# Recurrence of a hybrid decoder layer: chunks of 64 tokens per head in place of chunks of 32 per pair of heads

## What is computed

```python
def step(state, inp):
    r_t, w_t, k_t, v_t, a_t, b_t = inp
    sa = jnp.einsum('bhvk,bhk->bhv', state, a_t)
    state = (state * w_t[:, :, None, :] + sa[..., None] * b_t[:, :, None, :]
             + v_t[..., None] * k_t[:, :, None, :])
    y_t = jnp.einsum('bhvk,bhk->bhv', state, r_t)
    return state, y_t
...
y = rwkv7_recurrence(r_h, hs(decay), k_mod, v_h, -kk, kk * alpha_h)
mean = jnp.mean(y, axis=-1, keepdims=True)
var = jnp.mean(jnp.square(y - mean), axis=-1, keepdims=True)
y = ((y - mean) * lax.rsqrt(var + GN_EPS) * f(ln_x_w).reshape(RWKV_HEADS, HEAD_DIM)
     + f(ln_x_b).reshape(RWKV_HEADS, HEAD_DIM))
bonus = jnp.sum(r_h * k_mod * f(r_k), axis=-1, keepdims=True) * v_h
return (y + bonus).reshape(bsz, t_len, RWKV_WIDTH) * g
```

## Time and profile before

| | us |
|---|---|
| three executions | 2338.67, 2337.99, 2333.99 |
| their median | 2337.99 |
| span of the profiled execution | 2329.1 |
| the median less that span | 8.9 |
| busy in the span: TensorE | 2231.0 (96%) |
| VectorE | 1756.5 (75%) |
| ACT | 1141.8 (49%) |
| GpSimd | 1025.4 (44%) |

### The profile page before, as it was taken

One profiled execution on the slowest core, in us unless ns is written; L12 is line 12 of the kernel. 1 busy time (PEld: TensorE's weight loads), 2 busy tenths in 40 slices (PEclk: granted clock), 3 DMA queues, 4 the chain that ended last, 5 costly groups with the idle time before them and its releaser, 6 DMA issues.

```text
span 2329.1 us, 43634 instructions
## 1 busy us (share of the span) xinstructions
PE 2231.0 (96%) x16652; PEld 1816.6 (78%) x16652; DVE 1756.5 (75%) x1910; ACT 1141.8 (49%) x1795; POOL 1025.4 (44%) x726
## 2 busy tenths in 40 slices
PE   7999999996999979998999999999999999999998
PEld 6777777775878768887888888788788888887886
DVE  3756798994884466769989999666799898976565
ACT  5646556452445554444444444454554444444543
POOL 4636466571234335535776766100146555541000
PEclk9999999998999989999999999999999999999999
DMA  7364556347567547895434343677733332326774
GB/s 203 93 227 134 178 160 209 106 140 216 154 166 194 144 144 234 268 279 166 153 119 147 121 146 128 217 252 255 237 119 115 104 111 93 113 95 202 247 260 145
DMA packets 435819, 395.61 MB, mean 170 GB/s; under 512 B 59548, under 2 KB 352076, under 8 KB 432332
## 3 DMA queue, kind: packets, MB, share of 16 engines
q1 hardware_dynamic: 407804, 343.06, 47.8%
q10 hardware_dynamic: 27856, 50.34, 6.0%
HBM read 266.97 MB, written 126.35 MB: 169 GB/s over the span
## 4 chain that ended last, share of the span: by engine, by line
PE 55%; DVE 3%; DMA 2%; ACT 1%; issue 1%; SPq 0%; ACTq 0%; POOLq 0%; POOL 0%; DVEq 0%
PE late_bank L133 18%; PE late_bank L134 18%; PE late_bank L135 18%; DVE wt_lo L2906 1%; DMA scratch_a<-p_keep 1%; ACT wt_hi L2727 1%; PE late_bank L2199 1%; DMA o_lo<-scratch_q 0%; DVE wt_lo L2860 0%; DMA p_keep<-in_w_down 0%; DMA raw<-in_w_down 0%; DMA scratch_x<-x_tile 0%; DMA p_keep<-scratch_td 0%; DVE p_ub L2869 0%; DVE x_tile L2168 0%
## 5 line engine op out<-in xcount | busy, mean ns | idle before, releaser
L133 PE MATMUL late_bank<-o_hi,wt_hi 128*128 128x512 f32 x1232 | 481.3, 391 | 8.0 <-DVE o_lo L2962 3.3
L134 PE MATMUL late_bank<-o_lo,wt_hi 128*128 128x512 f32 x1232 | 480.7, 390 | 0.0
L135 PE MATMUL late_bank<-o_hi,wt_lo 128*128 128x512 f32 x1232 | 480.6, 390 | 0.0
L431 POOL TENSOR_TENSOR p_w_lo<-p_w_raw,p_w_hi 128x1024 fp32r<-128x1024 f32 x72 | 190.4, 2645 | 221.2 <-ACT p_w_hi L502 221.2
L133 PEld LDWEIGHTS late_bank<-o_hi,wt_hi 128*128 128x128 f32 x1232 | 232.0, 188 | 58.7 <-issue 7.2
L135 PEld LDWEIGHTS late_bank<-o_hi,wt_lo 128*128 128x128 f32 x1232 | 232.1, 188 | 48.8
L134 PEld LDWEIGHTS late_bank<-o_lo,wt_hi 128*128 128x128 f32 x1232 | 232.0, 188 | 47.8
L2597 POOL TENSOR_TENSOR tsum<-raw 128x512 f32<-128x512 f32 x43 | 106.2, 2469 | 358.5 <-DVE p_ub L2947 179.4
L133 PE MATMUL p_ppr<-p_hT_hi,p_w_hi 128*128 128x512 f32 x576 | 233.4, 405 | 0.2 <-ACT p_ring L513 0.2
L133 PE MATMUL late_bank<-wt_hi 128*128 128x512 f32 x572 | 223.2, 390 | 7.2 <-DVE wt_lo L2906 6.6
L135 PE MATMUL p_ppr<-p_hT_hi,p_w_lo 128*128 128x512 f32 x576 | 226.6, 393 | 0.0
(11 more groups left out here) (328 smaller groups left out, 4679.3 us busy)
## 6 DMA issues: line engine op xcount, KB each, us to landing
raw<-in_w_up SPq DMA_DIRECT2D x88, 512.0 KB, 5.1
p_w_raw<-in_w_in SPq DMA_DIRECT2D x72, 512.0 KB, 3.9
scratch_a<-p_keep SPq DMA_DIRECT2D x22, 1280.0 KB, 4.5
raw<-scratch_a SPq DMA_DIRECT2D x96, 256.0 KB, 3.0
raw<-scratch_td SPq DMA_DIRECT2D x52, 256.0 KB, 3.7
p_keep<-scratch_a SPq DMA_DIRECT2D x47, 256.0 KB, 2.9
scratch_a<-p_keep SPq DMA_DIRECT2D x44, 256.0 KB, 2.0
raw<-in_w_down SPq DMA_DIRECT2D x44, 256.0 KB, 4.1
```

The source lines that it names most:

```text
L133: nc.tensor.matmul(out, lhs_hi, rhs_hi, start=start, stop=False, skip_group_check=again)
L134: nc.tensor.matmul(out, lhs_hi, rhs_lo, start=False, stop=False, skip_group_check=again)
L135: return nc.tensor.matmul(out, lhs_lo, rhs_hi, start=False, stop=stop, skip_group_check=again)
L431: nc.gpsimd.tensor_tensor(w_lo[i][:, :, :], w_raw[i][:, :, :], w_hi[i][:, :, :].bitcast(F32), ALU.subtract).then_inc(s_wl, 1)
```

## The change

Chunks are 64 tokens long (`L = 2 * C`) and every product is of one head. The array is used as four tiles of 64x64: half h of the partitions into half h of a bank is an "own" tile, the other two go crosswise. The chain's step has one more link, since `w` is gone: `from_state` gives a S + A' v, ACT takes it as `pz`, the inverse is applied, ACT takes u, `to_state`. There are two such steps in an iteration for four. In each of them the chain's eight products (own tiles) come first and eight others (the cross tiles) right behind: k v into the state's bank, A'' v into y, the gram of r and k. VectorE's `advance` is an add and a multiplication by the decay in both steps. The inverse of 64 is put together from two of 32: X21 = X2 L21 X1, in `corner`, `corner_right` and `corner_left`, with ACT taking `l21`, `m1` and `x21`, and VectorE making a 32x32 `transpose` x1u.

Order of one iteration on TensorE:

```diff
                     if b:
-                        wait_read(pe, i - 1, "w1")
                         from_state(0)
+                    if o or a2:
+                        from_r_and_gram_of_a()
+                    if b or o:
+                        inverse_first()
                     if a2:
-                        bk_transposes(0)
...
+                        corner()
+                    if d:
+                        turn_y()
+                    if b or o:
+                        to_state_first()
                     if o:
-                        from_r(0)
...
+                        from_u()
                     if b:
                         from_state(1)
                     if a2:
-                        bk_transposes(1)
...
+                        corner_right()
+                    if b or a2:
+                        inverse_second()
                     if a2:
-                        bk_transposes(2)
...
+                        gram_of_b_and_turn_k()
+                    if b or a2:
+                        to_state_second()
                     if a2:
...
+                        turn_b_and_z()
+                        corner_left(0)
+                        corner_left(1)
```

The new products, 8 of each in a chain step and 16 of each in the interleaved groups:

```diff
+                    def from_state(c2):
...
+                        for j in range(PAIRS):
+                            for h in range(2):
+                                own = nc.tensor.matmul(pbank[half(h), c2 * PAIRS + j, :], ar[now][half(h), j, 0, tokens(c2)],
+                                                       st[p][c2][half(h), j, :], start=False, stop=True, skip_group_check=True)
+                        own.then_inc(s_as, 1)
+                        for j in range(PAIRS):
+                            for h in range(2):
+                                kv = nc.tensor.matmul(sbank[half(h), j, :], bkt[p][other(h), 1, (c2 * PAIRS + j) * H:(c2 * PAIRS + j + 1) * H],
+                                                      uv[now][other(h), 1, c2 * PAIRS + j, :], start=j == 0, stop=False, skip_group_check=True)
...
+                    def from_r_and_gram_of_a():
...
+                                for h in range(2):
+                                    if o:
+                                        own = nc.tensor.matmul(ybank[half(h), c2 * PAIRS + j, :], ar[old][half(h), j, 1, tokens(c2)],
+                                                               st[q][c2][half(h), j, :], start=c2 + j == 0, stop=False, skip_group_check=True)
+                                    if a2:
+                                        ak = nc.tensor.matmul(units(AB)[other(h), c2 * PAIRS + j, :], kinds[half(h), j, 1, tokens(c2)],
+                                                              ar[nxt][half(h), j, 0, tokens(c2)], start=True, stop=True)
```

GpSimd's body (the eight copies with padding are gone):

```diff
+                    if c:
+                        n = i - 2
+                        gp.wait_ge(s_mean, ONE + n + 1)
+                        nc.gpsimd.tensor_tensor(y[n % 3][:, :, :], y[n % 3][:, :, :], stat[p][:, 0, :].unsqueeze(2).to_broadcast([P, HEADS, H]),
+                                                ALU.add).then_inc(s_yc, 1)
...
+                        gp.wait_ge(s_yc, ONE + n + 1)
+                        nc.gpsimd.tensor_tensor(y2[:, :, :], y[n % 3][:, :, :], y[n % 3][:, :, :], ALU.mult).then_inc(s_sq, 1)
...
+                        nc.gpsimd.tensor_tensor(m[:, :, :], m[:, :, :], bg[n % 2][:, :, 0, :], ALU.add).then_inc(s_add, 1)
...
+                        nc.gpsimd.tensor_tensor(m[:, :, :], m[:, :, :], bg[n % 2][:, :, 1, :], ALU.mult).then_inc(s_mo, 1)
+                    if c:
+                        n = i - 2
+                        gp.wait_ge(s_rec, ONE + n + 1)
+                        nc.gpsimd.tensor_tensor(y[n % 3][:, :, :], y[n % 3][:, :, :], stat[p][:, 3, :].unsqueeze(2).to_broadcast([P, HEADS, H]),
+                                                ALU.mult).then_inc(s_yc2, 1)
```

ACT's square (L1459) is gone. VectorE's masks are three of 128x512, its solver has `GAPS = 6` and `TURNS = 5`, so 27 parts of a block lie in five iterations (i = 0 to 4 and 5 to 9). Loads, in `phase_recur`:

```diff
+                    for h in range(2):
+                        for e in range(2):
+                            sp.dma_start(xt[g][quad(h, e), :, C * e:C * e + C], whole[k, g, h, e]).then_inc(s_xl[n % 2], 16)
+                            for c in range(2):
+                                sp.dma_start(xd[n % 2][quad(h, c), e, :, :], parts[k, g, h, c, e]).then_inc(s_xl[n % 2], 16)
...
+                            sp.dma_start(rows(bk[n % 2]), group("bk", n)).then_inc(s_in[n % 2], 16)
+                            if n >= BATCH:
+                                sp.wait_ge(s_yd, ONE + 3 * (n - BATCH + 1))
+                            sp.dma_start(rows(ar[n % BATCH]), group("ar", n)).then_inc(s_in[n % 2], 16)
+                            spread(n)
```

b with k, a with r, and bonus with gate are now one load each, from scratch laid out by group; v has two loads an iteration, the turned a none. y has three buffers for two, the mix, bonus with gate, and the norm's statistics two for one. In `phase_project` the turned rows of a are not made:

```diff
-                        if f == 1 and b > 0:
-                            a_rows(b - 1, [pm[:, g, :] for g in range(TT)])
...
-                    if pair == 0 and b > 0:
-                        pe.wait_ge(s_abr, ONE + b)
-                        rows(dec, [pm[:, g, :] for g in range(TT)], s_atn)
...
-                rows(dec, LAST, s_atn)
```

More of the change, by code:

```diff
@@ L1273, in body @@
[L1273 to L1283 removed]
+                            sp.wait_ge(s_xz, ONE + BATCH + 1)
@@ new lines, in from_r_and_gram_of_a, with from_u @@
+                        if o:
+                            own.then_inc(s_yd, 1)
+                        if a2:
+                            ak.then_inc(s_gd, 1)
+                    def from_u():
+                        pe.wait_ge(s_yd, ONE + 3 * (i - 1) + 2)
+                        for c2 in range(2):
+                            for j in range(PAIRS):
+                                for h in range(2):
+                                    u = c2 * PAIRS + j
+                                    last = nc.tensor.matmul(ybank[half(h), u, :], ark[(i - 1) % 3][half(h), 0, c2, j, :], uv[old][half(h), 0, u, :],
+                                                            start=False, stop=True, skip_group_check=True)
+                        last.then_inc(s_yd, 1)
@@ new lines, in place_of, with corner @@
+                    def place_of(name):
+                        t, k = job(i, name)
+                        pe.wait_ge(s_read[t], ONE + k)
+                        return bank[:, ROT[t], :], s_full[t]
+                    def corner():
+                        at, full = place_of("l21")
+                        for j in range(PAIRS):
+                            for c2 in range(2):
+                                for h in range(2):
+                                    last = nc.tensor.matmul(at[quad(h, c2), j * C:(j + 1) * C], ar[nxt][half(h), j, 0, c2 * L + C:c2 * L + L],
+                                                            kinds[half(h), j, 0, c2 * L:c2 * L + C], start=True, stop=True)
+                        last.then_inc(full, 1)
@@ new lines, in corner_right @@
+                    def corner_right():
+                        wait_read(pe, i, "l21")
+                        at, full = place_of("m1")
+                        pe.wait_ge(s_xu, ONE + i + 2)
+                        for j in range(PAIRS):
+                            for c2 in range(2):
+                                for h in range(2):
+                                    last = nc.tensor.matmul(at[quad(h, c2), j * C:(j + 1) * C], l21[quad(h, c2), j, :], xd[q][quad(h, c2), 1, j, :],
+                                                            start=True, stop=True)
+                        last.then_inc(full, 1)
@@ new lines, in turn_y @@
+                    def turn_y():
+                        pe.wait_ge(s_yc2, ONE + i - 2)
+                        at, full = place_of("y")
+                        for j in range(PAIRS):
+                            for c2 in range(2):
+                                for h in range(2):
+                                    last = nc.tensor.matmul(at[half(h), j * SC + c2 * L:j * SC + c2 * L + L],
+                                                            y[(i - 3) % 3][half(h), c2 * PAIRS + j, :], ident[half(h), half(h)], start=True, stop=True)
+                        last.then_inc(full, 1)
```

825 lines of the change are left out of this document (373 added, 452 removed).

## The result

The changed kernel takes 2397.0 us in the median of four executions (2393.4 to 2401.0), the one before 2336.0 in its four; the ratio is 1.027, interval 1.0245 to 1.0292. The forecast was 2317 us, faster, and its range ended at 2350. The profiled execution is the slowest of the four with a span of 2399.2 us and 2401.0 us in all, so only 1.8 us lie around the span.

What follows compares the result with a forecast made beforehand. TensorE's product order was taken to bound later iterations, shared with VectorE in the solver's. Projection -5.4 - 0.7, start-up -0.9, iterations -16.5, tail +2 gave -21.5 from 2338.0: 2317 us, range 2281 to 2350.

Steps and rivals of the forecast that it cites:

- the sum's last term: 15 iterations: 9 us added, about 0.3 us an iteration of TensorE standing unreleased, plus 4 to 5 us of the first iteration.
- Waves, starts, overlap: 12.9 to 13.6 us: TensorE's iteration: 208 waves 12.1 us, 14 groups add 1.8, overlaps take back 0.35 to 1.0; 13.4 taken.
- The rival in which tiles don't run four at a time: Interleaved 64x64 pairs go in turn, 2.8 us an iteration come back: 2340 us, no change; chance 0.08.
- Row tiles on one bank: Rival in TensorE's products: diagonal pairs writing one bank go in turn, 8.7 us an iteration more, 2420 us; chance 0.02.
- The chain hides: Recurrence: two state steps of 4.1 us, 8.2 in all, hide in 13.4 us of TensorE work if VectorE takes updates at once.
- GpSimd and VectorE meet: Solver iterations: each solver step beside a GpSimd operation loses about 0.95 us; five meetings cost 4.7 us an iteration.
- the rival that ends slower: Solver iterations: VectorE waits behind GpSimd, broadcasts and square taking 2.4 to 2.65 us; 2352 us; chance 0.16.
- the 16.5 us of my sum: VectorE in a solver iteration: 6 + 5.1 + 4.7 = 15.8 us and some 0.7 of waiting between the norm's handovers.
- Projection, -6.1 us: Before the recurrence: removing the decay rows' transposes saves 5.4 us in three groups, 0.7 us in the fourth.
- Tail, +2: i = 16 and 17: the turn of y waits for GpSimd's weight conversions and norm operations; 0 to +4 us, +2 taken.
- The time around the span: Whole kernel: 8.9 us around the profiled span of 2329.1 us make the median 2338.0.
- SyncE's queue: Issues at about 0.6 us each: start-up -0.9 us, bounds -3 and +3; 9.6 us an iteration for 10.8.

Runs made afterwards that it cites:

- almost no data: Changed kernel with, from group 4 on, loads cut to 8 of 128 rows and inverse blocks to 1 of 32, all products kept: 2369.2 us, ratio 1.016.
- both cuts: Changed kernel with most cross-tile products left out from iteration 2 and loads cut to a few rows from group 4: 2322.1 us, ratio 0.996.
- 2 KB runs: Changed kernel with scratch laid out so the projection's stores have runs of 2 KB for 512 bytes, loads 512 bytes for 1 KB: 2382.9 us, ratio 1.021.
- both repairs: Changed kernel with all its work, scratch giving stores 2 KB runs, and loads of b, k, a, r in halves between short ones: 2369.8 us, ratio 1.015.

## Why the prediction was wrong

**The step that failed is the sum's last term**: "about 0.3 us an iteration more of TensorE standing with nothing to release it". I had counted the 544 records for 436 and seen the gap at 703.07, and gave it 0.3 us. Measured, TensorE's stands on issue are 68.5 us in the 15 iterations for 5.0 before, 4.2 us an iteration more, so that this term was sized at a fourteenth of what it is. That is 59 us over the forecast, where the 15 iterations missed it by 63; the other terms moved too, the meetings of VectorE and GpSimd down, the array's time at the lower clock up. The granted clock fell as well, from 0.98 to 0.85. I did not look at what separates such gaps. In the kernel before, the one at 703.07 comes 126 records behind the last, while the DMA engines are busy throughout:

```profile
698.22:703.05 4.83, 3.88 (x126) 1.00 0.99 284
```

Its 51 packets in 251.5 us, with so few stands, show a stream that just keeps up with products that take 4.9 us a portion. The change wants 63 portions in the 235 us of my forecast, 3.7 us each. Single ones came in as fast, as the stretch of 3.67 us above, but no kernel here was served so over its iterations: even with almost no data it was 4.25 us, which makes 268 us of 63 portions, more than the 251.5 before. The change puts four tiles to work at once, and so uses up its instructions fastest just where it saves time.

Point by point:
- *Waves, starts, overlap: 12.9 to 13.6 us.* Borne out as the array's work, not as a period: with all products and almost no data TensorE is busy for 13.2 us an iteration, at a clock of 0.92 (197.5 us in 15). The groups were miscounted, 21 for 17 before and 15 for 14 after, which brings the sum for the kernel before closer to its 15.45 us and adds 0.1 us to the one after. Followers do start early: in the changed kernel's timeline at 801.16 the state's own products begin, the followers at 801.45, and the next group at 801.75. The rival in which tiles don't run four at a time falls.
- *Row tiles on one bank.* The rule of the Trainium skill, TensorEngine Tiling (Array Packing), Restrictions and Gotchas, that different row tiles cannot access one PSUM bank simultaneously, shows in no time here: of the 16 and 16 products of `from_r_and_gram_of_a`, own and cross tiles together, 63 of the 64 records start in 0.94 us, from 802.78 to 803.72, 16 waves at 58 ns.
- *The chain hides.* Right as far as it was put to the test: the chain's products wait for ACT for 0.2 us in all 15 iterations. But they had 19.9 us an iteration to hide in; with both cuts, at 14.9, it is 0.5 us. The 4 to 5 us that I gave the first iteration were right too: one wait for VectorE of 8.3 us, for 3.7 before.
- *GpSimd and VectorE meet.* Right in mechanism and size per meeting. In the changed kernel's timeline, VectorE's solver and then GpSimd:

```profile
698.10 1.15 DVE L1442 TENSOR_TENSOR prod<-solve 128x150 f32<-128x150 f32 x1
699.29 1.15 DVE L1444 TENSOR_TENSOR solve<-solve,prod 128x150 f32<-128x150 f32 x1
700.47 0.33 DVE L1442 TENSOR_TENSOR prod<-solve 128x168 f32<-128x168 f32 x1
```

```profile
698.04 1.04 POOL L1295 TENSOR_TENSOR p_y<-p_y,p_stat 128x512 f32<-128x512 f32 x1 [1.15 <-DVE p_stat L1496]
699.23 1.04 POOL L1300 TENSOR_TENSOR p_squares<-p_y 128x512 f32<-128x512 f32 x1
```

  1.15 us beside a GpSimd operation, 0.33 without. 34 of the solver's 120 operations take over 0.8 us for 5 before. The broadcast operations take 1.04 us, so the rival that ends slower falls as well: the kernel did end at its side, but by another cause, since with the solver gone the iterations are hardly shorter (19.5 for 20.1). Behind the first iteration TensorE waits for VectorE in no row of the 15, so the meetings cost at most about these 0.6 us. Whether a solver iteration would have taken the 16.5 us of my sum is not shown: it took 15.2 with both cuts, with fewer products.
- *Projection, -6.1 us.* With 2 KB runs the recurrence starts at 536.3 us for 548.7, -12.4. Of that, 5.0 us are stands on issue ahead of the products of a and b at the end of a block, 8.5 us in the kernel before and 3.5 with the 2 KB runs, which I had not read. But I costed the stores' new layout at nothing. It is the second step that failed, +27 us, and its rows were the issue times of ACT's queue, 1.42 us for the store of b in 2 KB runs. They would not have told the price of short runs; they would have told that there is a price.
- *Tail, +2.* The mechanism was the one named; the size was off, +7.0. The turn of y stands for GpSimd, 6.8 us in two waits in this stretch, and stands on issue take 3.1 more; before, it waited 1.9 us for VectorE. The group's line over the whole kernel (busy, mean ns, then idle time before and its releasers):

```profile
L1763 PE MATMUL late_bank<-p_ident,p_y 64*64 64x64 f32 x512 | 24.6, 262 | 13.7 <-issue 6.9 <-POOL p_y L1317 6.8
```

- *The time around the span.* The 8.9 us between the profiled span of before and the median were taken as a constant; after, they are 1.8 us beside its own execution. An execution of the kernel before with the same span of 2329.1 us is on record with 2331.1, 2.0 us around it. So they were mostly the distance of one execution from another, and the 70 us between the spans are 61 between the medians.
- *SyncE's queue.* Four loads of v in 2.78 us are 0.70 us each, not 0.6. The start-up came out at -2.4, within its bounds.

Open: which part of the 298 us is the stands themselves and which the low clock. They are not one thing: with both repairs the stands are as long as with the 2 KB stores alone (73.3 for 69.7) and the clock is higher (0.89 for 0.82), and the iterations are 14 us shorter. But no run changes one of them and nothing else. The rest of the kernel is 4.0 us longer by the cut at the last turn of y; that was not followed up.

## What to carry to other kernels

Before a change that replaces wide products by more and smaller ones, look for stands on "issue" that recur at a fixed count of records, and count the packets of instructions in the DMA view. In a stretch with many such stands, its time by its packets is about the price of a portion, and the new number of packets at that price is the time to expect, whatever the array gains. In a stretch with few of them, as in the kernel before, the quotient is only an upper bound on that price: it can't forecast the loss, but it warns that the stream has been served no faster than that. And a store's price is also the time for which it holds the queue of the engine that issues it; where runs get shorter, read the rows of stores that follow one another.

## What the runs showed of the hardware

- TensorE's instructions come in packets of 16 KB, some 253 counted instructions each. Where TensorE stood on issue for over 20 us in 15 iterations, one took on average 4.6 to 5.0 us with the usual loads (4.7 in the changed kernel) and 4.25 us where nearly all of them were cut.
- 54 products of 32x32, which occupy TensorE for 1.1 us, cost 55 us of the kernel in 14 iterations; five of 128x128, which occupy it for 1.3 us, cost 18 us.
- A 1 MB store issued from ACT right behind another one of the same kind took ACT's queue 6.15 us with 512-byte runs and 1.43 us with 2 KB runs; one ahead of which ACT issued none for 15 us took 0.54 us with either.
- Products on the four 64x64 tiles, two and two of them writing one bank, ran at 58 ns a wave of four records: 63 records in 0.94 us.
- After a stand of 3.2 us a group of 16 waves took 1.98 us, with the granted clock at 0.70 in that stretch.
